# Gating of the retention output on GpSimd: ten multiplications in place of two

## What is computed

```python
def retention_out(o, g):
    mu = jnp.mean(o, axis=-1, keepdims=True)
    var = jnp.mean(jnp.square(o - mu), axis=-1, keepdims=True)
    on = (o - mu) * lax.rsqrt(var + EPS)
    return (on * jax.nn.silu(g.astype(jnp.float32))).astype(g.dtype)
```

## Time and profile before

| | |
|---|---|
| median of three runs | 1596.8 us |
| the profiled execution | 1597.14 us |
| its span | 1595.6 us |
| TensorE busy | 1571.7 us, 99% of the span |
| VectorE busy | 783.5 us, 49% |
| ScalarE busy | 565.6 us, 35% |
| GpSimd busy | 387.9 us, 24% |
| mean granted clock | 0.996 of full speed |

### The profile page before, as it was taken

How to read it: one execution, slowest core, us unless ns; L and a number is a source line. 1 busy time by engine, 2 the same in 40 slices (tenths; PEclk the granted TensorE clock), 3 DMA queues, 4 the chain that set the end, 5 groups by cost and what they waited for, 6 DMA issues and landing times.

```text
span 1595.6 us, 27497 instructions
## 1 busy us (share of the span) xinstructions
PE 1571.7 (99%) x10810; PEld 1497.5 (94%) x10810; DVE 783.5 (49%) x1022; ACT 565.6 (35%) x888; POOL 387.9 (24%) x421
## 2 busy tenths in 40 slices
PE   9999989999999999999999999999999999999998
PEld 6899879999999999999988997799999999999997
DVE  3324786665543245553322248857554522555522
ACT  4332266245552123322222323643455411333312
POOL 3370020432221012222306402115222200221223
PEclk9999999999999999999999999999999999999998
DMA  5321253222322223322233213612233232232222
GB/s 199 123 76 54 93 186 140 77 99 96 129 97 92 86 90 109 105 67 77 71 102 123 86 47 135 231 59 72 94 130 105 86 102 89 94 129 79 65 73 92
DMA packets 44415, 161.99 MB, mean 102 GB/s; under 512 B 5793, under 2 KB 8257, under 8 KB 43265
## 3 DMA queue, kind: packets, MB, share of 16 engines
q1 hardware_dynamic: 39680, 129.70, 25.0%
q0 software_dynamic: 2464, 28.26, 4.4%
q10 hardware_dynamic: 2208, 3.15, 0.5%
HBM read 149.08 MB, written 30.88 MB: 113 GB/s over the span
## 4 chain that ended last, share of the span: by engine, by line
PE 89%; DVE 6%; ACT 2%; issue 2%; POOL 1%; POOLq 0%; DVEq 0%; ACTq 0%
PE PSUM L1490 62%; PE PSUM L1540 13%; PE PSUM L1565 6%; PE PSUM L1466 4%; PE PSUM L1780 1%; DVE RS L987 1%; PE PSUM L1718 1%; PE PSUM L1556 0%; PE PSUM L1713 0%; DVE SM L1195 0%; ACT WH L728 0%; ACT PS L799 0%; POOL YT L691 0%; DVE XNL L1357 0%; DVE CT L1392 0%
## 5 line engine op out<-in xcount | busy, mean ns | idle before, releaser
L982 DVE TENSOR_TENSOR WL<-RAW,WH 128x1024 fp32r<-128x1024 f32 (+1 forms) x216 | 294.4, 1364 | 489.1 <-ACT WH L728 488.6
L728 ACT ACTIVATE WH<-RAW 128x1024 fp32r<-128x1024 f32 (+1 forms) x216 | 211.9, 982 | 553.9 <-PE PSUM L1490 385.9
L1490 PE MATMUL PSUM<-XFH,WH 128*128 128x320 f32 x1056 | 240.9, 310 | 1.8 <-DVE WL L982 1.2
L1490 PE MATMUL PSUM<-XFH,WL 128*128 128x320 f32 x1056 | 240.0, 309 | 0.0
L1490 PE MATMUL PSUM<-XFL,WH 128*128 128x320 f32 x1056 | 240.0, 309 | 0.0
L1490 PE MATMUL PSUM<-XNH,WH 128*128 128x320 f32 x864 | 198.2, 310 | 1.0 <-DVE XNL L1357 1.0
L1490 PE MATMUL PSUM<-XNL,WH 128*128 128x320 f32 x864 | 196.8, 309 | 0.0
L1490 PE MATMUL PSUM<-XNH,WL 128*128 128x320 f32 x864 | 196.7, 309 | 0.0
L1490 PEld LDWEIGHTS PSUM<-XFH,WH 128*128 128x128 f32 x1056 | 176.2, 188 | 3.0 <-issue 2.7
L1490 PEld LDWEIGHTS PSUM<-XFL,WH 128*128 128x128 f32 x1056 | 176.3, 188 | 0.0
L1490 PEld LDWEIGHTS PSUM<-XFH,WL 128*128 128x128 f32 x1056 | 176.2, 188 | 0.0
(11 more groups left out here) (230 smaller groups left out, 2341.5 us busy)
## 6 DMA issues: line engine op xcount, KB each, us to landing
RAW<-w_gu SPq DMA_DIRECT2D x88, 512.0 KB, 3.5
RAW<-w_in SPq DMA_DIRECT2D x40, 512.0 KB, 3.6
RAW<-w_down SPq DMA_DIRECT2D x32, 384.0 KB, 3.0
RAW<-w_down SPq DMA_DIRECT2D x32, 320.0 KB, 2.7
CAK<-ca_kt SPq DMA_DIRECT2D x16, 512.0 KB, 4.6
CAV<-ca_v SPq DMA_DIRECT2D x16, 512.0 KB, 5.1
RAW<-w_out SPq DMA_DIRECT2D x16, 512.0 KB, 3.6
ca_kt_copy<-ca_kt POOLq DMA_DIRECT2D x16, 512.0 KB, 4.9
```

Source lines behind the costliest of these rows:

```text
L728: nc.scalar.activation(WH[:, s, 0:width], RAW[:, s, 0:width], ACT.Copy).then_inc(hi_ready[s], 1)
L982: nc.vector.tensor_tensor(WL[:, s, 0:width], RAW[:, s, 0:width], WH[:, s, 0:width].bitcast(F32), ALU.subtract).then_inc(lo_ready[s], 1)
L1490: last = nc.tensor.matmul(PSUM[:, b + a, 0:HALF], w[:, s, P * k:P * (k + 1)], x[:, HALF * a:HALF * (a + 1)], start=start and k == 0 and w ...
```

## The change

The last two multiplications of the block, one over the four prompt blocks at once (1536 columns) and one over the sample block (384 columns), become ten: for each of the five blocks one over the first two slots (256 columns) and one over the third (128 columns). The products are the same, in the same place, and the signal is still raised by the last one.

```diff
                 ret_scaled.wait(pool, l, "scaled")
-                for blocks in (slice(0, SAMPLE), slice(SAMPLE, BLOCKS)):
-                    o = T[:, blocks, ret_slots(blocks.start), :].rearrange("p b s n -> p b (s n)")
-                    last = nc.gpsimd.tensor_tensor(o, o, T[:, blocks, RET_G:RET_G + 3, :]
-                                                   .rearrange("p b s n -> p b (s n)"), ALU.mult)
+                for b in range(BLOCKS):
+                    for half in (slice(0, 2), slice(2, 3)):
+                        o = T[:, b, ret_slots(b), :][:, half, :]
+                        last = nc.gpsimd.tensor_tensor(o, o, T[:, b, RET_G:RET_G + 3, :][:, half, :], ALU.mult)
                 ret_gated.done(last, "gated")
```

## The result

The changed kernel took 1594.83 us (median of 22 runs, 1594.1 to 1596.17) beside 1597.1 us for the kernel before (22 runs, 1596.05 to 1599.4). The ratio is 0.9985, with an interval of 0.9979 to 0.9992: 2.3 us less, against 2.6 forecast, inside the range, and inside the 0.2% that the prediction counted as no change. The profiled execution took 1594.78 us, 1593.2 of it the span, against 1597.14 and 1595.6.

The account below looks back on a forecast made before the run. TensorE, busy 99% of the span, was taken as the bound, losing time to waits and a lowered clock. Gains of 2.3 us in layer 0 and 0.3 in layer 1 made 2.6: 1594.2 us against the 1596.8 median, range 1592.8 to 1596.4.

Parts of the forecast that it names:

- waits of L1245 and the copies (1.2 us): VectorE, layer 0: L1245 and three copies each wait half a small GpSimd multiplication, 0.3 us, four waits in all.
- lead behind the copies: VectorE, layer 0: how much earlier it is after the copies; 2.71 us from L1195 less 1.2 of waits, 1.5 us.
- slack of 0.8: Layer 0: exponentials' last accumulator read by 222.42, TensorE's last transposes near 223.2; 0.8 us added to the lead.
- the lowered clock: TensorE, layer 0, at 213 to 214: granted clock 0.50 after idling, costing 1.43 us in transposes and score products.
- TensorE's own limit (1.98 + 1.43 us): Layer 0: the most TensorE could win, its wait for L1293 plus the slow-clock loss, 3.4 us.
- cap by the keys in layer 0: TensorE, layer 0: keys used from 218.56, second half near 218.8, land near 215.6, capping the shift at 3.2 us.
- rival A: Copies get through with one wait in all; lead 2.4 us or more, 3.5 us gained, 1593.3 us; chance 0.22.
- Layer 1: 0.3 us forecast: TensorE keeps at most 0.2 us of its 1.05 us wait and saves up to 0.24 later; range 0 to 0.45.
- cap by the last keys: Layer 1: the keys' second half, issued at 996.8, lands at 1003.4, so TensorE keeps at most 0.2 us.
- B: Rival: gating does not cause the stall, or an equal one replaces it; within 0.5 us, 1596.5 us; chance 0.10.
- C: Rival: small multiplications cost far more than the line through the two sizes, up to 1.42 us; 1607 us; chance 0.05.
- D: Rival: L1195 is held to the end of all ten multiplications, 2.1 us more per layer, 1601 us; chance 0.02.

Follow-up runs that it names:

- e1: The kernel before with its two gating multiplications unchanged but started only after VectorE's six copies; 1594.23 us, ratio 0.9978 to the kernel before.
- e3: The kernel before with its two gating multiplications swapped, 384 columns first and 1536 second; 1596.23 us, ratio 0.9989 to the kernel before.
- e4: The kernel before with the gating left out, retention output not multiplied by its gate; 1595.42 us, ratio 0.9983 to the kernel before.
- e6: The kernel before with the gating cut into fifteen multiplications of 128 columns; 1595.22 us, ratio 0.9974 to the kernel before.
- e7: The kernel before with its wide multiplication cut behind the third block (1152, 384 and 384 columns); 1597.72 us, ratio 0.9991 to the kernel before.
- e11: The kernel before with only the window keys' load (SWK) moved behind that of the last cached keys; 1598.72 us, ratio 1.0 to the kernel before.
- e12: The kernel before with fourteen unused spare products on TensorE in layer 0's gap; 1598.07 us, ratio 1.0 to the kernel before.
- e5: e1 with the window keys' load (SWK) moved behind that of the last cached keys; 1594.71 us, ratio 0.9973 to the kernel before.
- e8: e2 with the window keys' load (SWK) moved behind that of the last cached keys; 1593.79 us, ratio 0.9967 to the kernel before.
- e10: e8 measured again, unaltered, on one chip with e9; 1593.01 us beside 1598.64 us for the kernel before, ratio 0.9967.
- e9: The changed kernel measured again, unaltered; 1595.07 us beside 1598.64 us for the kernel before, ratio 0.9977.
- e2: The changed kernel with VectorE's six copies placed one unit later; 1594.26 us, ratio 0.9973 to the kernel before.

## Why the prediction was right, and where it was off

**The mechanism held.** L1195 takes 0.70 us as forecast, in both layers, the multiplications 0.73 and 0.46, the ten of them 5.57 against 5.5, and the work on GpSimd stays hidden. e1, e3, e4, e6 and e7 show the wait as a function of one thing, the length of the GpSimd instruction beside it.

**The waits of L1245 and the copies (1.2 us) were too low.** I took three copies of six and half a multiplication each. Four wait, back to back, each for what is left of the one beside it: 0.48 + 0.18 + 0.45 + 0.19 over their 0.22, and L1245 0.19: 1.5 us. The lead behind the copies is then 216.43 - 0.27 - 214.96 = 1.2 us in place of 1.5 (0.27 us is how much sooner L1195 starts in the profile after). With the slack of 0.8 that makes 2.0, which is what layer 0 gained; 2.3 was forecast. A copy that comes right behind one that has waited comes at the start of the next piece, not at its middle. (L1267 behind L1195 is the exception: it passed.)

**The 0.8 us of slack behind the exponentials held**, as lead + slack gives the gain of layer 0 to the tenth, and the 0.36 us wait for L782 stands where the prediction had put the limit. But the slack is the lowered clock itself, seen from behind. In e3, e7, e11 and e12 VectorE's lead over before, measured from the start of the stretch to L1182 behind the copies, is 1.0, 1.0, -0.2 and -0.9 us, and each gains that lead + 0.8; with the clock up, TensorE waits 0.35 to 0.36 us for L782 in all four. TensorE had slack in the profile of before because the clock had made it late.

**TensorE's own limit (1.98 + 1.43 us) did not decide,** and so a fault in it stayed hidden: it took the lowered clock as part of every execution. e11 shows it absent after a longer gap. Against an execution whose clock stays up, the gain of layer 0 would be 1.2 us and not 2.0. How many executions of the kernel before have the fall at 213 isn't known.

**The cap by the keys in layer 0 was set too high.** The forecast let TensorE be 3.2 us early there. The products with the last keys did start 3.3 us sooner in the stretch, but those with PTS only 2.7, since the second half of the keys was late. It didn't count, as the exponentials allowed 2.0 only. For rival A it would have: e1, whose copies do not wait, stops at 2.8.

**Layer 1: 0.3 us forecast, 0.05 found** (0.77 in the stretch, less 0.72 in front of it). The cap by the last keys is where it was placed, as e5, e8 and e10 show by lifting it. The issue of these keys kept its place 0.1 us behind the start of the stretch (994.9 and 996.4), as the step assumed. Up to the products with PTS TensorE kept 0.34 us, where at most 0.2 were allowed, and behind them it saved 0.43, where 0.24 were. What the step did not have at all are the keys of unit 2, which were late ahead of the stretch and took the 0.72. That wait is 0.4 us in the profile of before and 1.1 to 1.5 in all others but e12, where it is 2.1; e11 (1.1) and e12 have the stall and still wait. So the change does not bring it; the profile of before was at the low end.

**Luck in the sum.** The total (2.6 forecast, 2.3 found) is close because the profile of before, from which it was worked out, has two things that are not in every execution and that pull apart: the lowered clock, which adds 0.8 us to the gain, and the short wait for keys, which takes 0.7 from it. Beside the runs of the kernel before in e9 the gain is 3.6 us, at the upper bound of 3.65.

**The rivals.** A, copies that pass: false, four of six took 0.4 to 0.7 us in place of 0.22. The Trainium skill ("SBUF — State Buffer", section "Who interferes with whom") has such a copy held until GpSimd's instruction is done; by that rule the lead was put at 1.5 us and not 2.4, and the trace agrees, with 1.2. B, the stall has another cause: false by e1, e2 and e4. In one sense it had a point: in e4 another wait, 0.86 us for values, did take its place in part, though in that execution alone. C, dear small instructions: 0.46 us for 128 columns, not 1.42. D, held to the end of all ten: false, VectorE came in behind the first.

**What stays open.** Why the keys of unit 2 in layer 1, and the values in e4, land up to 1 us apart from one execution to the next. What decides that L1267 passes where a copy is held. And what brings the clock down: TensorE had waited 1.98 us in one stretch where it fell (before, layer 0) and 2.06 in another (e12, layer 1), and 2.20 (e11) and 1.00 (e7) in two where it did not.

## What to carry to other kernels

In these traces a long elementwise instruction on GpSimd held VectorE for its whole length when VectorE came with two inputs from SBUF (3.40 us beside one of 3.44) or a copy within it (0.70 beside one of 0.73), L1267 excepted: look in the view by line for small instructions whose longest execution is many times their median, and for a GpSimd instruction that ends with them. The cure is to put the GpSimd work where VectorE reads PSUM (L1230 and L1281 took 0.76 and 0.40 us beside the ten pieces, as they do without them), or to cut it; cutting caps each wait but multiplies their number, so count the instructions of VectorE that fall into the lengthened stretch, each as lasting up to a whole piece. And count the gain up to the next limit only: TensorE's own loss was 1.98 + 1.43 + 1.05 = 4.5 us, of which 2.3 came back in these two profiles; the copies, the exponentials and loads that were just in time took the rest. Moving one load, worth nothing before, was part of the last 2 us afterwards.

## What the runs showed of the hardware that was not expected

The granted clock did not follow the length of the gap: 1.00 behind 2.20 us of idle TensorE in e11, 0.50 behind 1.98 us in the kernel before and behind 2.06 us in layer 1 of e12. And the hold on VectorE is as tight as the records can tell: the addition ended 0.01 us behind the multiplication of 3.44 us, and in e6 it took 0.42 us where a piece of 0.46 had started 0.05 us ahead of it.
